# The even mixer of a 512-token, float32 block: position bias added by products in PSUM, softmax scaling on GpSimd, all convolution taps on VectorE, layer sums as products

## The reference

```
u = rmsnorm(h) @ w_in                      # q: 8 heads x 64, k and v: 2 heads x 64, glu: 2 x 512
scores = q.k / 8 + rel_bias[bucket(dist)]  # window of 128: a block of 128 queries sees 256 keys
probs = softmax(concat(scores, sink))[..., :-1]
attn = probs @ v                           # 8 heads -> 512 channels
glu = u[..., o3:o4] * sigmoid(u[..., o4:]) # 512 channels
c = silu(layernorm(causal_conv31(glu)))    # 31 taps per channel, then mean and variance over 512 channels
h = h + concat(attn, c) @ w_out
```

## Time and profile before

| | us |
|---|---|
| median of 3 timed runs | 3262.34 (3257.78, 3262.34, 3262.51) |
| profiled execution, its own time | 3256.76 |
| its span, first to last instruction | 3255.0 |
| PE busy | 3038.1 (93%) |
| DVE, ACT, POOL busy | 1622.0, 1203.1, 583.2 |
| mean granted clock of PE | 0.957 |

### The profile page before, as it was taken

How to read it: one execution, slowest core, us unless ns; L and a number is a source line. 1 busy time by engine, 2 the same in 40 slices (tenths; PEclk the granted TensorE clock), 3 DMA queues, 4 the chain that set the end, 5 groups by cost and what they waited for, 6 DMA issues and landing times.

```text
span 3255.0 us, 37398 instructions
## 1 busy us (share of the span) xinstructions
PE 3038.1 (93%) x13536; PEld 2468.3 (76%) x13536; DVE 1622.0 (50%) x1904; ACT 1203.1 (37%) x1602; POOL 583.2 (18%) x528
## 2 busy tenths in 40 slices
PE   7999989889999998899998789999999997799998
PEld 6888767768788886688886368888888885588886
DVE  7664355487566534534339744333333344743432
ACT  5553251378455424322231243222322223532221
POOL 1111110235211111211129311110111101111110
PEclk9999999889999999999999589999999998899999
DMA  4222232100222222222232012222222231122222
GB/s 165 93 99 84 93 112 80 52 1 1 78 101 92 83 99 95 74 94 93 87 104 80 0 52 91 103 82 97 106 98 95 80 110 56 65 97 97 94 85 79
DMA packets 47018, 272.63 MB, mean 84 GB/s; under 512 B 5920, under 2 KB 7760, under 8 KB 24528
## 3 DMA queue, kind: packets, MB, share of 16 engines
q1 hardware_dynamic: 46928, 271.42, 23.9%
HBM read 269.29 MB, written 2.11 MB: 83 GB/s over the span
## 4 chain that ended last, share of the span: by engine, by line
PE 83%; DVE 10%; ACT 4%; issue 2%; POOL 1%; DMA 0%; POOLq 0%; SPq 0%; DVEq 0%; ACTq 0%
PE bank L451 26%; PE bank L453 26%; PE bank L452 26%; DVE cy L1883 2%; DVE w_lo L1421 1%; PE bank L738 1%; ACT probs L1195 1%; DVE rc L2036 1%; POOL sq_sum L2131 1%; ACT w_hi L950 0%; PE bank L854 0%; PE bank L650 0%; PE bank L464 0%; DVE rs L1427 0%; PE bank L754 0%
## 5 line engine op out<-in xcount | busy, mean ns | idle before, releaser
L451 PE MATMUL bank<-h_hi,w_hi 128*128 128x512 f32 x2624 | 1040.8, 397 | 100.6 <-DVE w_lo L1421 52.9
L452 PE MATMUL bank<-h_lo,w_hi 128*128 128x512 f32 x2624 | 1030.4, 393 | 0.0
L453 PE MATMUL bank<-h_hi,w_lo 128*128 128x512 f32 x2624 | 1029.6, 392 | 0.0
L1421 DVE TENSOR_TENSOR w_lo<-w_raw,w_hi 128x2048 fp32r<-128x2048 f32 (+2 forms) x283 | 577.4, 2040 | 616.4 <-ACT w_hi L950 615.8
L451 PEld LDWEIGHTS bank<-h_hi,w_hi 128*128 128x128 f32 x2624 | 497.8, 190 | 220.5 <-DVE w_lo L1421 68.5
L950 ACT ACTIVATE w_hi<-w_raw 128x2048 fp32r<-128x2048 f32 (+2 forms) x283 | 476.7, 1684 | 342.7 <-PE bank L453 308.0
L452 PEld LDWEIGHTS bank<-h_lo,w_hi 128*128 128x128 f32 x2624 | 498.1, 190 | 106.9 <-issue 3.5
L453 PEld LDWEIGHTS bank<-h_hi,w_lo 128*128 128x128 f32 x2624 | 497.5, 190 | 106.0
L451 PE MATMUL bank<-act_hi,w_hi 128*128 128x512 f32 x1056 | 411.6, 390 | 7.1 <-DVE hid L1547 4.7
L452 PE MATMUL bank<-act_lo,w_hi 128*128 128x512 f32 x1056 | 410.8, 389 | 0.0
L453 PE MATMUL bank<-act_hi,w_lo 128*128 128x512 f32 x1056 | 410.8, 389 | 0.0
(11 more groups left out here) (287 smaller groups left out, 2950.0 us busy)
## 6 DMA issues: line engine op xcount, KB each, us to landing
w_raw<-in_w_up SPq DMA_DIRECT2D x132, 1024.0 KB, 4.9
w_raw<-in_w_down SPq DMA_DIRECT2D x96, 704.0 KB, 4.0
w_raw<-in_w_wout SPq DMA_DIRECT2D x12, 1024.0 KB, 4.9
w_raw<-in_w_ple SPq DMA_DIRECT2D x16, 640.0 KB, 3.9
w_raw<-in_w_ein SPq DMA_DIRECT2D x6, 1024.0 KB, 5.0
w_raw<-in_w_kproj SPq DMA_DIRECT2D x4, 1024.0 KB, 4.9
w_raw<-in_w_qproj SPq DMA_DIRECT2D x4, 1024.0 KB, 4.9
w_raw<-in_w_rec SPq DMA_DIRECT2D x4, 1024.0 KB, 5.1
```

Of the source, the lines that this page charges most:

```text
L451: pe.matmul(out, wh, mh, start=first, stop=False)
L452: pe.matmul(out, wh, ml, start=False, stop=False)
L453: return pe.matmul(out, wl, mh, start=False, stop=final)
L1421: dve.tensor_tensor(w_lo[j % 2][:, 0:n], w_raw[j % 2][:, 0:n], w_hi[j % 2][:, 0:n].bitcast(F32), ALU.subtract).then_inc(w_lo_done, 1)
```

## The change

- The bias is split into `eb_hi` (ACT, scaled by 8) and `eb_lo` (DVE), and PE adds both to the scores in PSUM, as products with an identity `ident_r`, before q.k. DVE's maxima read PSUM, and ACT's exponentials read PSUM too; DVE's scale-and-add goes.
- k is kept as `kz`, v as `vz`, one copy for each half of the 128 rows or columns with the other half zero, so that q.k is 128 rows deep and p.v 128 columns wide. p.v covers two query tiles with one product of 256 columns. Transposes go four and three to a bank; ACT keeps 512 and 384 columns at once in three buffers `eturned`.
- The scaling by the softmax factor is on POOL, in the two-operation form that the first block's attention has.
- All 120 taps are on DVE, chunks in pairs, 10 a job, 8 and 4 around einv, five and five in a unit between the maxima.
- The layer sums accumulate four products each over `cy` and over the squares; POOL's sums go. They stand after PE's units 7 and 9 (before: one product each, after 5 and 7).
- wout1 takes output chunks in fours: for each four, first the convolution's input chunks (4 to 7), then the attention's (0 to 3).

```
-LN_AT = (5, 7)
+E_SPANS = (4 * P, 3 * P)
+LN_AT = (7, 9)
@@ PE @@
-                    pe.matmul(bank[t][:, 0:n], eq[rows, r, t * P:(t + 1) * P], eq[rows, 4, lo:lo + n],
-                              start=True, stop=True).then_inc(qk_done, 1)
+                        pe.wait_ge(exp_done, 5 * (u - 1) + t + 1)
+                    out = bank[t][:, 0:n]
+                    pe.matmul(out, ident_r[:], eb_hi[:, u, cols], start=True, stop=False)
+                    pe.matmul(out, ident_r[:], eb_lo[:, u, cols], start=False, stop=False)
+                    pe.matmul(out, eq[:, r, t * P:(t + 1) * P], kz[:, half, lo:lo + n], start=False, stop=True).then_inc(qk_done, 1)
...
+                def layer_sums(i):
+                    if i == 0:
+                        pe.wait_ge(rs_col_done, 2)
+                        pe.wait_ge(y_tap, CC * (TAPS - 1))
+                    else:
+                        pe.wait_ge(ln_vec, CC)
+                    for c in range(CC):
+                        if i:
+                            pe.wait_ge(ln_sq, c + 1)
+                        mm = pe.matmul(bank[LN][:], ones[:], (cy[:, c], squares_of[c])[i], start=c == 0, stop=c == CC - 1)
...
+            def even_output():
+                for pair in range(2):
+                    for part, chunks in enumerate((range(CC, ND), range(CC))):
+                        for n in range(4 * pair, 4 * pair + 4):
...
+                                mm = three(bank[n % 4][:], *tile_of(j % 2, n % 2 * ND + k), e_hi[:, k], e_lo[:, k],
+                                           part == 0 and k == CC, part == 1 and k == CC - 1)
@@ ACT @@
                 split_w(J0["wout1"])
+                for i in range(4):
+                    act.wait_ge(flipped, i + 1)
+                    act.activation(eb_hi[:, 2 * i:2 * i + 2].rearrange("p h s -> p (h s)"), bank[5 + i % 2][:], ACT.Copy,
+                                   scale=1.0 / QK_SCALE).then_inc(bias_hi, 1)
@@ DVE @@
-                todo = [(1, tap) for tap in range(TAPS - 1)] + [(c, tap) for tap in range(TAPS - 1) for c in (2, 3)]
+                todo = [(2 * pair + i, tap) for pair in range(2) for tap in range(TAPS - 1) for i in range(2)]
...
-                        conv_taps(8)
+                        conv_taps(10)
...
+                for u in range(E_UNITS + 4):
+                    now = u < E_UNITS
+                    if now:
+                        maxima(u, (0, 1))
+                    conv_taps(5)
+                    if u >= 5 and u % 2 == 1:
+                        keep_o((u - 5) // 2)
+                    if now:
+                        maxima(u, (2, 3))
+                    conv_taps(5)
+                    if now:
+                        factor(u)
@@ POOL @@
-            def convolution_branch():
+            def even():
+                pool.wait_ge(h_lo_done, H_COUNT["mixe"] + 1)
+                pool.memset(kz[:], 0.0).then_inc(zeroed, 1)
+                pool.memset(vz[:], 0.0).then_inc(zeroed, 1)
+                for u in range(E_UNITS):
+                    pool.wait_ge(fac_done, 2 * u + 2)
+                    for t in range(NT):
+                        e = eprobs[u % 3][:, t, P if t == 0 else 0:]
+                        pool.tensor_scalar(e, e, estat[:, u % 2, 3, t:t + 1], 1.0, ALU.mult, ALU.mult).then_inc(e_norm, 1)
```

More of the change, by code:

```diff
@@ L199, in build @@
             eprobs = [sb(f"eprobs{i}", [P, NT, 2 * P], to=part) for i in range(3)]
+            eturned = [sb(f"eturned{i}", [P, 7 * P], to=part) for i in range(3)]
         h_hi = sb("h_hi", [P, ND, T], F32R)
@@ L836, in turn @@
[L836 to L844 removed]
+                    cols = slice(2 * P - n, 2 * P)
+                    if u == 0 and t == 0:
+                        pe.wait_ge(bias_kept, 4)
+                        pe.wait_ge(ident_kept, 1)
+                        pe.wait_ge(k_kept, 2)
+                        pe.wait_ge(v_kept, NT)
+                        pe.wait_ge(zeroed, 2)
@@ L845, in turn, with pv @@
                     mm.then_inc(turned, 1)
-                def pv(u, t):
+                def pv(u, x):
                     r, half = u // 2, u % 2
-                    out = bank[6][half * HD:(half + 1) * HD, t * P:(t + 1) * P]
-                    if half == 0 and t == 0 and r:
+                    if half == 0 and x == 0 and r:
                         pe.wait_ge(o_lo_done, ND + r)
-                    pe.wait_ge(kept_a, 4 * u + t + 1)
-                    for b in range(0 if t else 1, 2):
-                        mm = pe.matmul(out, ev[:, t - 1 + b, half * HD:(half + 1) * HD],
-                                       hid[:, t % 2, b * P:(b + 1) * P], start=(b == 0 or t == 0), stop=b == 1)
-                    mm.then_inc(pv_done, 1)
@@ new lines, in even_output @@
+            def even_output():
+                stage = "wout1"
+                for pair in range(2):
+                    for part, chunks in enumerate((range(CC, ND), range(CC))):
+                        for n in range(4 * pair, 4 * pair + 4):
+                            j = J0[stage] + n // 2
+                            if part == 0:
+                                pe.wait_ge(w_lo_done, j + 1)
+                                if pair:
+                                    pe.wait_ge(x_ready, x_before("up3") + n - 3)
+                            for k in chunks:
+                                if pair == 0 and n == 0:
+                                    if part == 0:
+                                        pe.wait_ge(ln_lo, k - CC + 1)
+                                    else:
+                                        pe.wait_ge(o_lo_done, ND + k + 1)
+                                mm = three(bank[n % 4][:], *tile_of(j % 2, n % 2 * ND + k), e_hi[:, k], e_lo[:, k],
+                                           part == 0 and k == CC, part == 1 and k == CC - 1)
+                            if part:
+                                mm.then_inc(seg_done, 1)
@@ L928, in _ @@
                 elif stage == "wout1":
-                    pe.wait_ge(ln_lo, 4)
-                    for q in range(4):
-                        dense(stage, q, e_hi, e_lo, o_lo_done, ND, residual="up3", chunks=4)
+                    even_output()
                 elif stage == "wout2":
@@ L1919, in even @@
                     conv_taps(1)
-                dve.wait_ge(bias_kept, 4)
                 split_w(J0["wout1"])
-                def bias(u, t):
-                    cols = slice(P if t == 0 else 0, 2 * P)
-                    if u >= 3 and t == 0:
-                        dve.wait_ge(turned, 4 * (u - 2))
-                    dve.wait_ge(qk_done, 4 * u + t + 1)
-                    dve.scalar_tensor_tensor(out=eprobs[u % 3][:, t, cols], in0=bank[t][:, 0:P if t == 0 else 2 * P],
-                                             scalar=QK_SCALE, in1=ebias[:, u, cols], op0=ALU.mult, op1=ALU.add)\
-                        .then_inc(scaled, 1)
@@ L1958, in keep_o, with factor @@
+                def factor(u):
+                    st = estat[:, u % 2]
+                    dve.wait_ge(exp_done, 5 * (u + 1))
+                    if u >= 2:
+                        dve.wait_ge(e_norm, 4 * (u - 1))
+                    dve.tensor_tensor(st[:, 2], st[:, 2], st[:, 0], ALU.add).then_inc(fac_done, 1)
+                    dve.wait_ge(fac_done, 2 * u + 1)
+                    dve.reciprocal(st[:, 3], st[:, 2]).then_inc(fac_done, 1)
                 def keep_o(r):
@@ L2245, in _ @@
                 elif stage == "ein":
-                    convolution_branch()
+                    even()
                 elif stage == "rec":
```

273 lines of the change are left out of this document (123 added, 150 removed).

## The result

The changed kernel took 3234.60 us in the median of four runs (3232.55 to 3236.64), the kernel before 3260.06 in four runs beside it (3256.38 to 3262.51): a ratio of 0.9925, 95% interval 0.9912 to 0.9937. That is 25.5 us less; the forecast was 3231, and its sum was 30.5. So the time came out inside the range of 3218 to 3250, 3.6 above the forecast.

The account below looks back on a forecast made before the run. Bound: 126 us of units and tail where PE is neither full nor fast, and six of ein. 34.7 gained by wout1's start less 4.2 in wout1 makes 30.5: 3226.3 profiled, 3231.8 as median, stated 3231; range 3218 to 3250.

Parts of the forecast that it names:

- Part 1, ein: In ein, faster taps on DVE nearly close PE's two gaps and remove the half-clock stretch: 7.0 us gained.
- Part 2: From ein to the first unit: `diag` near 1754, weights split by 1765.9, first q.k at 1772.8, first maxima at 1775.6.
- The chain of flips and remainders: Before the first q.k, copies, remainders, two flips at 2.08 and handovers for pairs three and four take 6.9 us.
- Part 3, the pace: In the units DVE sets the pace: 8.5 us for unit 0, 9.5 from unit 1 on.
- The price of GpSimd: In the units POOL's four scalings cost DVE 1.0 us a unit, between 0 and 1.8.
- Does PE keep up?: In the units PE needs 12.1 us at half clock, 6.0 at full, against DVE's 9.5, so the clock decides.
- Part 3, the clock: PE runs at 2.4 GHz, granted clock mostly 1.00, for most of the units.
- My 1.5 for falls: In the units, 1.5 us added for clock falls after PE's idle gaps, putting unit 7's bound at 1844.2.
- Part 4, the tail: From 0.5 before the last bound to wout1's first product 25.2 us, layer sums 4.5 each; wout1 begins at 1869.2.
- Part 5, wout1: In wout1 late weight splits delay job 2 by 0.7, job 3 by 2.8, the next layer by 0.7: 4.2 us lost.
- a cold PE: Rival: PE stays at 1.2 GHz, 12.1 us a unit from unit 2; 4 us gained, 3258; chance 12 in 100.
- GpSimd as the bound: Rival: scalings of 4 us each make units 16 long; 29 us slower, 3291; chance 4 in 100.

Follow-up runs that it names:

- e8: Kernel before with all 120 taps on DVE, in pairs, GpSimd making only the two sums: 3250.7 us, ratio 0.9979.
- e7: e6 with ACT's bias copies ahead of the split of wout1's first job and 12 taps, not 8, on DVE meanwhile: 3211.0 us, ratio 0.9854.
- e1: Changed kernel with the p.v of a unit's first half moved behind the q.k of tiles 2 and 3 on PE: 3228.9 us, ratio 0.9901.
- e4: Changed kernel with ten more single-pass 512-column products on PE in each of units 1 to 6: 3233.1 us, ratio 0.9916.
- e5: e1 with the second layer sums ahead of the p.v of unit 6 on PE: 3223.3 us, ratio 0.9894.
- e11: Changed kernel with q.k multiplying only its head's 64 rows again, not 128: 3240.2 us, ratio 0.9945.
- e3: Changed kernel with each of GpSimd's four scalings made twice in the first six units: 3236.8 us, ratio 0.9927.
- e2: Changed kernel with wout1 in its old order, output chunk by output chunk, after all four convolution remainders: 3229.9 us, ratio 0.9907.
- e6: e5 with the attention's input chunks first in wout1 for output chunks 0 to 3, and weight splits and copies moved: 3212.3 us, ratio 0.9862.
- e9: e7 with the attention's input chunk 3 put after its chunks 0 to 2 for all four output chunks in wout1: 3207.3 us, ratio 0.9845.

## Why the prediction was right, and where it was not

- **Part 1, ein:** 7.1 against 7.0. Ten taps take 6.71, and gaps of 0.13 and 0.24 are left. e8 shows the gain comes from the taps alone.
- **Part 2:** `diag` within 0.2; the way through DRAM and the load took 1.0 longer, and the first maxima came 0.5 late. The chain of flips and remainders took 6.3, worked out as 6.9. The idle time that it left on DVE was worth 3 (e7).
- **Part 3, the pace:** 8.92 instead of 9.5. The price of GpSimd was 0.57 a unit, not 1.0, inside the bounds of 0 to 1.8, and a unit without it 8.36, not 8.5. That gained 2.5 by unit 5. The scalings themselves took 3.10 for four beside the taps, 0.9 for one of 256 columns and not near 0.5; in the units that cost nothing that shows, since their transposes come two units later.
- **Part 3, the step that failed** is "Does PE keep up?", which compared PE's total for a unit with DVE's. PE had time enough, between 5.4 and 0.8 in front of each of units 1 to 5; but I didn't walk through its list. The p.v that waits for DVE's remainder stood in front of q.k, and that remainder behind five taps. By it DVE idled 4.25 in unit 5 and 3.43 in unit 7, and e1 gives back 6.8. The overlap of PE with DVE, not the sum of either, was wrong. Of the 5.1 lost, 1.4 shows at the start of unit 7, because the faster units had hidden the rest, and 3.7 in unit 7.
- **Part 3, the clock:** I said mostly 1.00. It was 0.73 from the first maxima to the last bound: it fell after PE's idle times and rose again in bursts that have seven transposes in them, as in the first attention. The units stayed at 8.92 all the same, at 0.73 as at 0.89 (e4). PE's real price at half clock was lower than mine: I priced q.k at 1.15 from a product 64 deep, and it takes 0.85 at 128. Unit 3, at 0.60, took PE 8.10 (1802.29 to 1810.39), where I had 12.1. That the forecast of the pace survived a wrong clock is luck: the error in the clock and that in the price cancelled. My 1.5 for falls has no measured counterpart; e4 gained 1.9 by the bound, of which a part is the difference between executions.
- **Part 4, the tail:** 26.9 from the end of the bound to wout1 instead of 25.0. (The terms of that sum add up to 25.7, which makes 25.2 from the bound, not 25.0.) Each set of sums took 3.6 to 3.8, not 4.5, but the second stood behind a p.v that waited 3.26 for the third remainder: the same ring, missed again (e5: 3.6).
- **Part 5, wout1:** waits of 0.75, 2.50 and 0.75, forecast 0.7, 2.8, 0.7. The length grew by 5.05, not 4.2: 4.0 are these waits, 0.3 a longer start at half clock (the first twelve products take 4.97 instead of 4.70), and the rest mostly the products next to each wait, which are further apart than 0.23.
- **The rivals:** a cold PE didn't come about, and e11 shows how near it was: with q.k 64 deep PE is busy for 62.5 of 77.4. GpSimd as the bound was far off (e3): doubling its work costs 0.3 a unit.
- **The sum and the forecast:** the gain was put at 30.5; by the two traces, counted from the common zero, it was 22.7, and by the runs side by side 25.5. The time came out only 3.6 above the forecast because the base helped: the kernel before took 3260.06 beside the change, 2.3 less than the 3262.34 that I forecast from. That the distance is so small is in part luck. The differences between executions are of the same size: in the traces the mixer begins anywhere from 1683.92 to 1689.49. Of the parts of the change only the taps (e8), the depth of q.k (e11) and the order of wout1 (e2) were run alone; how the rest of the gain divides among the bias products, GpSimd's scaling and the layer sums isn't shown.

## What to carry to other kernels

Don't ask whether an engine has time enough in a loop; walk through its list and write behind each wait what stands queued there. Here two waits of PE, 4.75 and 1.90, had q.k queued behind them, and moving p.v behind q.k gave back 6.5. When a norm's chain ends a stage, start the next stage's product with the inputs that are ready (e6 and e9: 10.4 and 5.6); e9 ran in 0.984 of the time before, twice the gain of the change.

## What the runs showed of the hardware

- A product 64 deep between ones 128 deep takes 0.62 instead of 0.43 at full clock (256 columns, float32), and the product in front of it is slower too: 1.05 instead of 0.76 for the tile. Neither its own weight load nor the next one runs ahead under the running product (e11).
- A scaling on GpSimd beside taps on DVE: for 1.73 of GpSimd's work DVE loses 0.57 and GpSimd 1.37; with the scalings doubled a unit is 0.3 longer (e3).
- PE's granted clock differs between executions of the same code in the stretches where PE is idle now and then: 0.73 in the change and 0.79 in e2, whose code is the same up to there. A shift of 2.5 at the layer norm's reciprocal goes with it; that the clock is its cause isn't shown.
